# Sample 0's compressed pages pooled beside the projection, its scores beside the prompt, and keys and values loaded apart

## The reference

```python
q, kc, vc, ks, vs, kw, vw, g, z = jnp.split(u, cuts, axis=-1)      # u: projection of the normed input
kc, vc, c_end = compressed_kv(kc rows, vc rows, ...)               # pooled blocks of 32 tokens, stride 16, then a small MLP
p_c = masked_softmax(q . kc);  o_c = p_c @ vc                      # compressed branch
imp = p_c.sum(3) @ overlap;    top_idx = top_k(imp + forced, 16)   # 16 of 65 blocks of 64 tokens
o_s = softmax over the chosen blocks (ks, vs);  o_w = softmax over the last 512 tokens (kw, vw)
o = g0 * o_c + g1 * o_s + g2 * o_w;  y = (o * silu(z)) @ w_out
```

## Time and profile before

| | us |
|---|---|
| median of 3 runs (1231.11 to 1237.3) | 1231.68 |
| the profiled execution | 1234.1 |
| its span, first to last instruction | 1232.4 |
| last matmul of the projection ends | 661.9 |
| first output tile (sample 0) begins | 991.0 |
| last output tile (sample 7) begins | 1189.2 |

### The profile page before, as it was taken

The page is one execution under the profiler, slowest core; times in us unless marked ns, Lnnn a source line. Parts: engine busy times, 40 slices in busy tenths (PEclk is TensorE's granted clock), DMA queues, the critical chain, the costliest instruction groups (busy, mean ns, idle before and its releaser), DMA issues. The chain is left out here.

```text
span 1232.4 us, 25152 instructions
## 1 busy us (share of the span) xinstructions
PE 1163.0 (94%) x9077; PEld 732.1 (59%) x9077; DVE 488.1 (40%) x1500; ACT 425.1 (34%) x1079; POOL 203.6 (17%) x345
## 2 busy tenths in 40 slices
PE   3899999999999999999998999999999599999995
PEld 1677774676767757477876555555555244544552
DVE  2444032344532421112203665656566323443445
ACT  3322112233321321010111565665656234444453
POOL 0000000000000102011102222222223524444300
PEclk9899999999999999999899999999999989999998
DMA  9654435303054302125004787667666999999972
GB/s 381 277 205 171 165 137 189 137 1 137 1 210 154 128 10 76 70 76 191 5 1 146 278 273 246 223 222 242 226 216 224 304 315 341 357 356 356 351 275 78
DMA packets 96551, 238.76 MB, mean 194 GB/s; under 512 B 12714, under 2 KB 50732, under 8 KB 91948
## 3 DMA queue, kind: packets, MB, share of 16 engines
q1 hardware_dynamic: 73036, 164.95, 38.1%
q0 software_dynamic: 23392, 72.21, 16.4%
HBM read 227.57 MB, written 17.05 MB: 198 GB/s over the span
## 5 line engine op out<-in xcount | busy, mean ns | idle before, releaser
L407 PE MATMUL ps<-arena,wring 128*128 128x288 f32 x1408 | 361.8, 414 | 2.0 <-ACT arena L547 2.0
L407 PEld LDWEIGHTS ps<-arena,wring 128*128 128x128 f32 x1408 | 266.8, 193 | 84.2 <-issue 12.3
L1721 POOL DMA_DIRECT2D arena<-in_cmp_pages x128 | 69.8, 546 | 269.8 <-PE ps L1886 100.0
L418 PE MATMUL ps<-wring,arena 128*128 128x512 f32 x192 | 90.1, 604 | 0.0
L1814 DVE CUSTOM_DVE_ANT_0 wring<-ps,wring 128x128 f32<-128x128 f32 (+3 forms) x128 | 57.6, 487 | 72.1 <-PE ps L1743 70.7
L2291 DVE CUSTOM_DVE_ANT_1 arena<-ps,small 128x512 f32<-128x512 f32 x64 | 44.2, 692 | 92.8 <-PE ps L2208 92.7
L1806 ACT ACTIVATE wring<-ps 128x128 f32<-128x128 f32 (+3 forms) x128 | 49.0, 436 | 86.6 <-PE ps L1766 86.6
L2267 ACT ACTIVATE arena<-arena 128x512 f32<-128x512 f32 (+1 forms) x88 | 57.0, 649 | 50.3 <-DVE arena L2307 50.3
L1792 ACT ACTIVATE wring<-wring 128x128 f32<-128x128 f32 (+3 forms) x128 | 70.7, 559 | 8.3 <-DVE wring L1814 8.3
L2278 ACT ACTIVATE arena<-ps 128x512 f32<-128x512 f32 x72 | 43.0, 597 | 81.7 <-PE ps L2229 81.7
L1879 PE MATMUL ps<-arena 128*32 128x256 f32 x1024 | 69.5, 389 | 0.4 <-DMA arena<-in_cmp_pages 0.4
(11 more groups left out here) (392 smaller groups left out, 1597.7 us busy)
## 6 DMA issues: line engine op xcount, KB each, us to landing
wring<-in_weights SPq DMA_DIRECT2D x27, 2048.0 KB, 10.1
arena<-in_cmp_pages POOLq DMA_DIRECT2D x128, 256.0 KB, 4.4
arena<-in_cmp_pages SPq DMA_DIRECT2D x128, 256.0 KB, 3.6
wring<-in_kv_pages SPq DMA_DIRECT2D x64, 256.0 KB, 11.3
wring<-in_kv_pages POOLq DMA_DIRECT2D x64, 256.0 KB, 7.1
arena<-in_kv_pages SPq DMA_DIRECT2D x50, 256.0 KB, 8.8
arena<-in_kv_pages POOLq DMA_DIRECT2D x50, 256.0 KB, 7.0
out_win_k_out<-in_win_kv SPq DMA_DIRECT2D x8, 512.0 KB, 12.1
```

The costliest lines, as they stand in the source:

```text
L407: last = pe.matmul(out[:, 0:HT], w[:, k, ct * P:ct * P + P], moving[k][:, half * HT:half * HT + HT], start=(k == 0), stop=(k == KT - 1))
L418: last = pe.matmul(main, tokens, w[:, k, :], start=(k == 0), stop=(k == KT - 1))
L1721: eng.dma_start(cring[q % CR][:, 2 * half + j, :], v["cmp_pages"][bass.ds(ids[2 * d + j], 1)] .rearrange("o p c -> (o p) c")).then_inc(c_i ...
```

## The change

One block of instructions holds all stages, so the barrier after the projection goes. Sample 0's compressed pages are pooled between the last projection units (two calls after each of units 25 to 28, into the two banks of one set, while the last eight units use the two other sets), one of its two turns of rows and the first half of the prompt's compressed scores stand there too. The filling is shifted by one unit (`i // SU + 1`), and the loop over nine steps more is gone. Seven of sample 0's scores stand in unit 7, three in the steps after it. Keys and values of a page are loaded by DMAs of their own: sample 0's keys go into the slots of the compressed pages as these come free, its values into the same places as the keys are scored; then SP and POOL alternate, a group of four DMAs of values of sample n, a group of four of keys of sample n+1. Each such group reads its four page numbers itself.

```diff
+        late_sets = end_a + [chunk for chunk, _, _ in plan_c].index(W_ZC)
...
+            if u >= late_sets:
+                return 2 - (u - late_sets) % 2
...
+                if i == len(plan_c) - 1 and k == 5 and half == 0:
+                    pe_rows_turn(pe, 0, 0)
+            def after_unit(i):
+                if i == len(plan_c) - 2:
+                    pe.wait_ge(act_p, AC2["vcs"])
+                    pe.wait_ge(dve_p, DV2["kcT"])
+                    prompt_cmp_scores(pe, 0)
+                prompt_compressed(i)
+                if len(plan_c) - 5 <= i < len(plan_c) - 1:
+                    for g in range(2):
+                        pe_pool(pe, 0, 2 * (i - len(plan_c) + 5) + g)
...
+        def page_slot(q):
+            return q % 2 if q < NG else q % CR
...
-                if q >= CR:
-                    eng.wait_ge(pe_c, PC_["pool", (q - CR) // NG, (q - CR) % NG])
+                if q in (NG + 2, NG + 3):
+                    eng.wait_ge(proj_done, u0c + len(plan_c))
+                elif q >= 2:
+                    before = q - 2 if q < NG + 2 else q - CR
+                    eng.wait_ge(pe_c, PC_["pool", before // NG, before % NG])
...
+        def keys_home(n, i):
+            return k_homes[((n - 1) * NL + i) % KR] if n else first_k[i]
...
+        def wait_keys_home(eng, n, i):
+            at = (n - 1) * NL + i
+            if n == 0 and i < NG:
+                eng.wait_ge(pe_c, PC_["pool", NB - 1, NG // 2 + i // 2])
+            elif n == 0:
+                eng.wait_ge(pe_a, PE3["t", 3 * SU, 0])
+            elif at < 4:
+                eng.wait_ge(pe_a, PE3["t", tile_step[at - 4], 1])
+            elif at < 6:
+                eng.wait_ge(pe_a, PE3["pv", U - 1])
             elif at < KR:
+                eng.wait_ge(valued, page_homes.index(k_homes[at]) + 1)
+            else:
+                eng.wait_ge(scored, ((at - KR) // NL + 1) * NJ + (at - KR) % NL + 1)
...
-        def load_kv(eng, half, n, pair):
+        def load_keys(eng, half, n, pair):
             ids = page_ids(eng, 0, ((n * (NG // 2) + pair) * 2 + half) * GP)
             for d in range(2):
                 i = 2 * pair + d
+                wait_keys_home(eng, n, i)
                 for j in range(2):
+                    lo = (2 * half + j) * KVW
+                    eng.dma_start(keys_home(n, i)[:, lo:lo + KVW], page_of(ids[2 * d + j])[:, 0:KVW])\
+                        .then_inc(k_in[half][keys_sem(n, i)], 16)
+        def load_values(eng, half, n, pair):
+            ids = page_ids(eng, 0, ((n * (NG // 2) + pair) * 2 + half) * GP)
...
+        def pool_third(pool):
+            pool.wait_ge(outs, stored_in_c[0])
+            pool.wait_ge(roped, 12)
+            pool.wait_ge(pe_p, PE2["gates"])
+            for pair in range(NB * NG // 2):
+                load_cmp(pool, 1, pair)
+            load_window_values(pool, 0)
+            for pair in range(NG // 2):
+                load_keys(pool, 1, 0, pair)
+            for n in range(NB):
+                for pair in range(NG // 2):
+                    load_values(pool, 1, n, pair)
+                    if n + 1 < NB:
+                        load_keys(pool, 1, n + 1, pair)
+                if n:
+                    load_window_values(pool, n)
...
+        def pe_third(pe):
+            pe_rows_turn(pe, 0, 1)
+            prompt_cmp_scores(pe, 1)
+            for i in range(U + 3):
...
+                if i < U:
+                    pe_fill(pe, i // SU + 1, i % SU, "a")
+                if 1 <= i - (U - SU) <= INSIDE:
+                    pe_scores(pe, 0, i - (U - SU) - 1)
...
+                if i >= U:
+                    pe_scores(pe, 0, INSIDE + i - U)
```

More of the change, by code:

```diff
@@ L1733, in prompt_scores @@
             u, t, br = steps[i]
-            if i and not is_tile[i - 1] and u:
-                pe.wait_ge(act_c, AC_["hv", u - 1])
+            if not is_tile[i - 1]:
+                pe.wait_ge(act_c, AC_["hv", u])
             if tile_no[i]:
@@ new lines, in act_third, with cmp_exp @@
+        def act_third(act):
+            def cmp_exp(gp):
+                act.wait_ge(dve_a, DV3["cm%d" % gp])
+                act.activation(pc[:, gp], pc[:, gp], ACT.Exp).then_inc(act_a, AC3.one("cexp%d" % gp))
+            cmp_exp(0)
+            for i in range(U + 2):
+                if i < U:
+                    act_fill(act, i // SU + 1, i % SU, "first")
+                if 2 <= i < U + 2:
+                    prompt_turned(act, i - 2)
+                if i < U:
+                    act_fill(act, i // SU + 1, i % SU, "a")
+                if i < U and is_tile[i]:
+                    prompt_exp(act, i)
+                if i < U:
+                    act_fill(act, i // SU + 1, i % SU, "b")
+                if i == 5:
+                    cmp_exp(1)
+            for n in range(NB):
+                act_exp(act, n, 0)
+                for at in range(NJ):
+                    if at < LAST:
+                        act_exp(act, n, at + 1)
+                    act_turned(act, n, at)
+            act.wait_ge(f_summed, 1)
+            act.activation(f_std[:, 0:TP], ps[:, 0, :], ACT.Sqrt, scale=1.0 / D, bias=eps[:, 0:1]).then_inc(f_rooted, 1)
+            act.wait_ge(s_rows, 1)
+            for half in range(2):
+                rows = slice(half * NS, half * NS + NS)
+                last = act.activation(s_tok[rows, :], ps[rows, 2 + half, :], ACT.Copy)
+            last.then_inc(s_copied, 1)
+            act.wait_ge(s_summed, 1)
+            act.activation(f_std[:, TP:NT], ps[:, 4, 0:NS], ACT.Sqrt, scale=1.0 / D, bias=eps[:, 0:1]).then_inc(s_rooted, 1)
@@ L2458, in _ @@
-                pe_out_turn(pe, NB - 1)
-                pe.wait_ge(so_gated, NB)
-                for i in range(4):
-                    pe.wait_ge(last_in[i], 32)
-                    for k in range(2 * i, 2 * i + 2):
-                        for half in range(2):
-                            last = pe.matmul(ps[half * NS:half * NS + NS, 2 + half, :], zT[:, k, TP:NT],
-                                             last_w[2 * i + half][:, k % 2, :], start=(k == 0), stop=(k == KT - 1))
-                last.then_inc(s_rows, 1)
@@ L2467, in _ @@
-                pe.wait_ge(s_copied, 1)
-                for ct in range(4):
-                    last = pe.transpose(ps[:, 5, ct * P:ct * P + P], s_tok[:, ct * P:ct * P + P], ident)
-                last.then_inc(s_done, 1)
-                pe.wait_ge(s_squares, 1)
-                pe.matmul(ps[:, 4, 0:NS], ones, s_sum, start=True, stop=True).then_inc(s_summed, 1)
+                add_parts = pe_first(pe)
+                pe_between(pe, add_parts)
+                pe_second(pe)
+                pe_third(pe)
```

565 lines of the change are left out of this document (295 added, 270 removed).

## The result

The changed kernel takes 1240.62 us (median of 8 executions), the kernel before 1235.47 on the same chips: a ratio of 1.004, 95% interval 1.0022 to 1.0058. It is slower by 0.4%, where 0.6% faster was forecast, and lies just above the range's upper end of 1239.

A forecast was written before the change was run, and what follows sets the result against it. PE was taken to bound prompt and samples, thinning out between; POOL's issuing would then rule the samples. 974 + 207.7 + 43.2 = 1224.9 span, 7.5 us less than 1232.4; off the median, 1224.2 us. Range 1211 to 1239.

The forecast's parts named there:

- The front: Stretch from the projection to the first output tile: tile 0 begins near 974, 17 us earlier (bounds 968 to 982).
- The rival in which the front doesn't shrink: Delays in unit 7, projection pooling and unit 0 put tile 0 at 984 and the time at 1234; chance 0.12.
- The mechanism in the samples: In the samples, POOL's eight load groups of 3.68 us plus the window cost 30.25 us, more than PE's 27.93.
- PE at 27.9: In the samples, POOL keeps pace and PE stays the bound, giving 1212 us; chance 0.18.
- half speed: Loads of half the size move half as fast, a sample takes 58 us, time above 1400; chance 0.02.
- Tile 2 at 56.4 after tile 0: Sample 2's last keys land at 53.6 after tile 0; tile 2 follows scores 7 after 2.8 us, at 56.4.
- Five samples of 30.25: From tile 2 to tile 7, POOL's 30.25 us a sample rule, putting tile 7 at 207.7 after tile 0.
- The rival of dearer groups: In the samples, a POOL group costs 4.0 us or more and the change loses, 1239 us; chance 0.12.
- 43.2 from tile 7 to the end: The stretch from tile 7 to the end of the span stays at 43.2 us; nothing is late there.
- SP near, but below POOL: SP's queue in the samples: groups of 3.50 us with window and tile make 29.2 us a sample, below POOL.
- DMA has no room either: In the samples, 9.96 MB a sample take 29.2 us at 341 GB/s, so DMA has no room.
- The fetch: In each POOL group, 1.36 us in which POOL waits for nothing shown were taken as fetching page numbers.

The follow-up runs named there:

- e3: Changed kernel with half the columns of each page loaded, keys from sample 2 and values from sample 3 on, same loads and waits: 1241.9 us.
- e4: Changed kernel with POOL fetching the four page numbers of every value group from sample 1 on a second time: 1264.9 us.
- e1: Changed kernel with page numbers fetched once with the keys and kept in registers for the values, on both queues: ratio 0.9925 to the kernel before.
- e6: Changed kernel with page numbers kept in registers on POOL's queue only, SP fetching as in the changed kernel: 1237.1 us.
- e12: Changed kernel with page numbers kept, two load places swapped and the compares behind each fetch left out: ratio 0.9878 to the kernel before.
- e9: Changed kernel without the eight compare instructions behind each fetch of page numbers: ratio 0.9915 to the kernel before.
- e10: Changed kernel with sample 1's keys 6 and 7 put into places that sample 0's first two value steps leave: ratio 0.9995 to the kernel before.

## Why the prediction was wrong, step by step

- **The front**: right, and closer than it deserved. Tile 0 came at 975.1 for 974; the hidden layers at 682.7 and 933.0 stood forecast at 680.1 and 932.3, so sample 0's came 2.6 us late and the seven units took 1.9 us less. The late start lies in a stretch that the change doesn't touch: PE reached a run of projection units at 468.10, for 464.86 in the kernel before. The rival in which the front doesn't shrink is out.
- **The mechanism in the samples**: right. POOL's issuing replaces PE as the bound, at 3.70 us a group (forecast 3.68) and 30.3 us a sample (30.25). e3 and e4 show it, e1 with SP's queue cheapened too. The rivals of PE at 27.9 and of half speed are out.
- **The step that failed** is the sum behind it, short by 15.0 us: 1224.9 forecast for a span of 1239.9. Of these 1.1 are the front's. Three terms make up the rest: the landing of the value window, put at nothing (3.9), POOL's sample without its stalls (7.1), and the end (2.9).
- *Tile 2 at 56.4 after tile 0*: it was 60.3. PE took up scores 7 at 1028.66, forecast 53.6 + 975.1 = 1028.7, but that is luck: POOL's last load of these keys went out at 1022.98, 47.9 us after tile 0 for 49.2, and the keys were there 5.7 us later for 4.4. Behind them I let the tile follow 2.8 us later as in the earlier trace rows. Between them stands the value step of the window, whose load of 0.5 MB POOL issues after the last keys; it lands 8.5 us later and not 4.4. I had priced the window's issue, 0.81, and not its landing, for which the list of the kernel before had rows:

```profile
arena<-in_win_kv POOLq DMA_DIRECT2D x4, 512.0 KB, 8.3
...
wring<-in_win_kv POOLq DMA_DIRECT2D x4, 512.0 KB, 7.4
```

That is 2.3 us of waiting, and 1.6 more since the work behind the wait went slower: the scores took 1.98 where 1.08 is the rule. Behind the 2.29 us in which PE stood still the granted clock was 0.50, the lower of its two levels (1.2 GHz), where it is 1.00 (2.4 GHz) from 1028 to 1032 us:

```profile
1032.00:1034.80 2.80, 2.77 (x36) 1.41 (x38) 0.00 (x0) 0.00 (x0) 1.57 (x3) 0.50 1.07 351
```

- *Five samples of 30.25*: (1193.73 - 1035.38) / 5 = 31.67, 7.1 us too few in all. POOL's groups cost what they should; its program has another 1.2 us a sample in stalls, 6.0 of the 7.1, that no row read of the kernel before had shown. What is left, 1.1, fits later landings: ahead of tiles 3, 4 and 5 PE waits at scores 6 or 7, as forecast,

```profile
1063.05 1.98 PE L2271 MATMUL ps<-wring,arena 128*64 128x512 f32 x4 [2.56 <-issue]
...
1093.10 1.69 PE L2271 MATMUL ps<-wring,arena 128*64 128x512 f32 x4 [2.67 <-issue]
...
1124.71 1.08 PE L2271 MATMUL ps<-wring,arena 128*64 128x512 f32 x4 [2.14 <-issue]
```

and the trace's semaphores have POOL's keys landing just before it goes on, at 1062.96, 1093.01 and 1124.62, 7.1, 8.0 and 7.8 us after their issue where I took 4.4 from loads of another stage. The forecast's own slope, 4.8 us for each 0.1 us of a group, gives 7 us for the 0.15 that 1.2 / 8 makes. The rival of dearer groups thus came nearest, for another reason than the one given.
- *43.2 from tile 7 to the end*: 46.1. Tile 7 itself takes 8.16 (1.1 more than the earlier trace rows), behind a wait of 1.82 us and at a granted clock of 0.84 from 1193 to 1202 us; PE stands 0.93 us in the middle of a value step at 1212; the rest is spread over small waits. The 0.93 us are no sign of late values: e3, with half the bytes of these values, has the same gap behind the same matmul. The cause of that gap stays open.
- **SP near, but below POOL**: mis-sized, 31.05 for 29.2 (e6). It cost the forecast nothing, POOL being as late, but it is why a cure for POOL alone brings 3 us (e6) and a cure for both 15 (e1).
- **DMA has no room either**: half right. With the issuing cheapened the transfers went at 355 GB/s and had little room left, and in e12 they were late; up to then they were not the bound, as e3 shows. The Trainium skill, "DMA: Bandwidth & Descriptors", section "Where 436 GB/s comes from", gives about 358 GB/s as the memory's limit for one core. The 355 lie near it, but no run here shows a limit there: a sample's 9.96 MB in PE's own 27.9 us are 357 GB/s, and the first fortieth of the changed kernel's span moved 381. The same page's section "Bandwidth" has the rule to batch loads; it pointed the right way here, though not by its reason: the loads overlapped, and it was their issuing that had no room.
- **The fetch**: I called the whole 1.36 us the fetching of numbers. 0.95 of it are compares (e9). The sum did not hang on it, but the cure does.
- **What the sum did not hang on**: the row of 15.79 us holds two units of 32 matmuls of the profile each, and 8 groups at 3.50 for 3.68 us make 1.4 us a sample less and not 1.6. The forecast in us also started from a median of 1231.68 of three executions, where the eight beside the changed kernel gave 1235.47; 3.8 us of its miss of 16.4 lie there. The forecast gain of 0.6% against a loss of 0.4% doesn't depend on it.

What stays open is the nature of POOL's stalls, and whether all of the 0.2 us a sample between POOL's 31.46 and PE's 31.67 belongs to landing times, which no experiment tried.

## What to carry to other kernels

When a change splits loads, count what each costs the queue that issues it, with the fetch and the checks ahead of it, and set that against the time of a step: a queue that sat waiting for places before can become the bound with no byte more moved. Follow each load to its landing and to the step that needs it; the large one that is issued last is the one that is late. And if two loads use the same number, keep it: here this turned a loss of 0.4% into a gain of 0.75%, or 1.4% with one more wait moved out of the queue's head.

## What was not expected of the hardware

- A fetch of four numbers with its eight compares kept POOL 1.37 us, and 0.42 without the compares (e9).
- POOL stands some 1.5 us about every other sample, in the middle of a group, with nothing that the profile shows to wait for; the spacing of its windows was the same to 0.1 us with half the bytes (e3), and the stalls stood before the same loads in e1, e3, e4, e9 and e10.
- Loads of 128 KB moved as many bytes as those of 256 KB, 355 GB/s in e1 and 341 to 357 in the kernel before; a DMA share of 0.98 in the changed kernel still left room, as e1's 1.06 shows.
- Behind a wait of 2.3 us four of PE's score matmuls took 1.98 for 1.08, at a granted clock of 0.50.
